# Two output projections of an adaptive block as three products of rounded halves, with the row products dealt out two and four to a turn

## The chip, the cores and the metric

The kernel runs on one core of one Trainium2 chip. The metric is the device time of one execution in microseconds (us), lower is better. Before the change it is 4800.77 us, the median of three runs (4797.85 to 4803.23 us).

## The reference, cut to what matters

Two transformer-like blocks over 512 tokens of width 1024 in fp32. The stage that is changed lies in the first block: the end of the token mixer and, beside it, the second block's first modulation vector, which only depends on a conditioning vector.

```python
y_att = attend(q, k, v) @ lw['w_attn_o']            # 512x1024 @ 1024x1024
y_conv = conformer_conv(u, lw)                      # its own projection is done earlier
merged = jax.nn.sigmoid(ga) * y_att + jax.nn.sigmoid(gc) * y_conv
return merged @ lw['w_out']                         # 512x1024 @ 1024x1024
...
xs = xs + g1 * token_mixer(hx, lw, rope, k_c, v_c)
hx = modulate(rmsnorm(xs, norm2_g[l]), sh2, sc2)    # begins with the mean of squares of xs
xs = xs + g2 * peer_ffn(hx, lw)
...
mod = (jnp.dot(cond, ada_w[layer]) + ada_b[layer])  # second block: 6144 values, each a dot product of length 1024
```

## The kernel before, in words

Activations lie channel by token: a tile of [128 channels, 8 groups, 512 tokens]. A projection to 1024 channels is eight slabs, one for each group of 128 outputs; a slab is a 128x1024 piece of the weight (512 KB), and its product is eight matmuls of 128x512 that add up in one PSUM bank. Slabs stream through a ring of four slots (`slab_ring`), filled by SyncE: it asks for slab n when the product of slab n - 4 has ended. `slab_used` counts ended products, `taken` counts banks that have been read, and four banks are in turn. Blocks of the program end with a barrier over all engines.

The stage is the function `mix_out` (from line 975). It has two phases of eight slabs each:

- Phase one, slabs 0 to 7 (`w_attn_o`): PE multiplies the attention's output `s.o` (the tile `conv`) by a slab (line 241). DVE multiplies the bank by one gate (line 1026) and adds the other branch (line 1028), and so makes group i of the merged tile.
- Phase two, slabs 8 to 15 (`w_out`): PE multiplies the merged tile by a slab. DVE scales the bank and adds it to x (line 1032), ACT squares the new group of x (line 1009), and PE sums the squares over channels (line 994, one matmul per group, two slabs behind).

Beside it DVE computes the second block's modulation: 48 row products, each the dot product of a 128x1024 tile of the transposed weight with a broadcast vector (`dot_row`, line 474, 512 KB of weight each). The rows come through a ring of four slots of their own (`mix_rows`), asked for by ACT (`fetch_row`, line 467): ACT waits until the row product that last used the slot has ended, then issues the DMA. Before the change three row products stand behind each slab in both phases. When the last of them has ended, DVE adds a bias and forms four small gain tiles (lines 480 and 495), and the block ends. The next block (the experts) begins with a square root on ACT (line 1305).

All instructions are issued in the order of the code, engine by engine. In other stages of this kernel projections are already done with halves: ACT rounds a slab to fp32r (`round_slab`, line 255), GpSimd subtracts that from the slab (`split_slabs`, line 262), the source is rounded and split in the same way on ACT and DVE (lines 269 and 276), and PE makes three fp32r products for each of the eight matmuls (`fine`, line 290; `fine_pair`, line 445, does two slabs at once as the source's groups arrive). `high` and `low` hold two slabs each.

Of the kernel before, what the change touches and what calls it, by code (L numbers as in the profile page):

```python
# [13 lines left out]
F32 = mybir.dt.float32  # L14
# [121 lines left out]
class Program:  # L136
# [838 lines left out]
    def mix_out(self, s):  # L975
# [3 lines left out]
        columns = list(range(NMOD))  # L979
        each = NMOD // (2 * KT)  # L980
        with self.nc.Block() as block:
# [5 lines left out]
            def _(pe):  # L987
                self.slabs(pe, 0, KT, self.linear(pe, s.o))
                pe.wait_ge(merged.sem, merged.at(KT))
                product = self.linear(pe, s.gates[:, KT:2 * KT, :])  # L990

# [3 lines left out]
                for i in range(KT):  # L995
                    pos = base + KT + i
                    pe.wait_ge(self.landed[pos % SLOTS], 16 * (pos // SLOTS + 1))
                    pe.wait_ge(self.taken, pos - SLOTS + 1)
                    product(pos % SLOTS, i).then_inc(self.slab_used, 1)
                    if i >= 2:  # L1000
                        square_sum(i - 2)
# [3 lines left out]
            @block.scalar  # L1005
            def _(act):
                def square(k):
                    act.wait_ge(self.taken, base + KT + k + 1)
                    act.activation(self.squares[:, k, :], self.x[:, k, :], ACT.Square).then_inc(squared.sem, 1)
                for n in range(NMOD):  # L1010
                    self.fetch_row(act, s, self.d["ada"], columns, n)
                    k, rest = divmod(n - each * KT - ROW_SLOTS + 1, each)
                    if k >= 0 and rest == 0:
                        square(k)
                for k in range((NMOD - ROW_SLOTS - each * KT) // each + 1, KT):
                    square(k)
                act.activation(self.one_root, self.eps[EPS], ACT.Sqrt)

            @block.vector
            def _(dve):  # L1020
                def rows(i):
                    for n in range(each * i, each * i + each):
                        self.dot_row(dve, s, n, self.crow[:, 1, :], self.mod2[:, columns[n]:columns[n] + 1])
                for i in range(KT):
                    dve.wait_ge(self.slab_used, base + i + 1)
                    dve.tensor_tensor(s.gates[:, i, :], self.bank[:, (base + i) % SLOTS, :], s.gates[:, i, :], ALU.mult).then_inc(self.taken, 1)
                    dve.wait_ge(self.taken, base + i + 1)
                    dve.tensor_tensor(s.gates[:, KT + i, :], s.gates[:, i, :], s.gates[:, KT + i, :], ALU.add).then_inc(merged.sem, 1)
                    rows(i)
                for i in range(KT):  # L1030
                    dve.wait_ge(self.slab_used, base + KT + i + 1)
                    dve.scalar_tensor_tensor(self.x[:, i, :], self.bank[:, (base + KT + i) % SLOTS, :], self.mod[:, 2 * KT + i, 0:1], self.x[:, i, :],
                                             ALU.mult, ALU.add).then_inc(self.taken, 1)
                    rows(KT + i)
                self.second_gains(dve, 0)
        merged.close(KT)
        squared.close(KT)
        self.close_rows(len(columns))
# [1506 lines left out]
    def build(self):  # L2545
        nc, d = self.nc, self.d
        with self.ctx:
# [44 lines left out]
            with ExitStack() as first:  # L2592
# [50 lines left out]
                with ExitStack() as inner:  # L2643
                    own = self.sb("mix_rows", [P, ROW_SLOTS, D], scope=inner)
                    s.mring = [own[:, j, :] for j in range(ROW_SLOTS)]
                    self.mix_out(s)
                if self.stop == "mixed":
# [325 lines left out]
```

## Time and profile before

| | us |
|---|---|
| median of three runs | 4800.77 |
| the profiled execution's own time | 4784.22 |
| its span (first to last instruction) | 4782.4 |
| the stage `mix_out`, from its first matmul to the end of DVE's last small gain | 606.7 to 727.8 |

The profiled execution is 16.6 us shorter than the median. A page of the profile lists busy time by engine, then groups of instructions by line. In a row of a group, `out<-in` names the tiles written and read, `xN` the count, the number after it the mean duration in ns, and what stands last is the idle time of the engine just before these instructions with what ended it. In a row of the timeline the first number is the start and the second the time to the end of the piece, both in us; instructions of one line are merged. The engines are PE (matmul), PEld (its weight load), DVE (VectorE), ACT (ScalarE), POOL (GpSimd), SP (SyncE); ACTq is ACT's queue issuing a DMA. An fp32 product of 128x512 shows as two records.

### The profile page before, as it was taken

Reading aid. Unit: us, or ns where it says so; the run is one execution under the profiler, and the core shown is the slowest. Engines: PE = TensorE matmul, PEld = TensorE weight load, DVE = VectorE, ACT = ScalarE, POOL = GpSimd, SP = SyncE. Lnnn points to the kernel's source line nnn. Section 1 sums busy time; section 2 is a strip of 40 time slices with the busy share of each in tenths; the row PEclk is TensorE's granted clock in tenths of the full one; section 3 lists DMA queues with packets and bytes.
Section 4 is the critical chain, followed back from the end, with each engine's and each line's share of the span. In section 5 each row is a group of like instructions: output and inputs, shape, how many; then the busy total and the mean of one; then the engine's idle time right before and its main releaser. Section 6 shows DMA issues by size and latency. Waiting matters only on the chain. (4 is left out here: it accounts for less than half of the span.)

```text
span 4782.4 us, 43840 instructions
## 1 busy us (share of the span) xinstructions
PE 4091.6 (86%) x15066; PEld 2742.5 (57%) x15066; DVE 2880.8 (60%) x4184; ACT 1659.3 (35%) x2193; POOL 1417.4 (30%) x1231
## 2 busy tenths in 40 slices
PE   4988997987776776777979999978999999999995
PEld 3874543432222322323767876767777877778774
DVE  4895656565656656652454456367557475574786
ACT  2322402222212212221324322326445364453675
POOL 0430003666666666664423442310000000000000
PEclk8998998999998998998989999988999999999998
DMA  4225076999999999997212364208658585675895
GB/s 153 94 86 202 1 266 236 376 383 368 364 370 371 370 377 365 365 373 272 84 49 71 96 216 149 88 18 350 260 214 306 190 319 208 227 288 190 326 362 199
DMA packets 260055, 1148.00 MB, mean 240 GB/s; under 512 B 28833, under 2 KB 28833, under 8 KB 212513
## 3 DMA queue, kind: packets, MB, share of 16 engines
q0 software_dynamic: 150768, 549.00, 30.0%
q1 hardware_dynamic: 87216, 514.37, 29.6%
q10 hardware_dynamic: 21888, 82.24, 4.7%
q8 instruction: 111, 1.82, 0.1%
q14 instruction: 72, 0.58, 0.0%
HBM read 1131.33 MB, written 14.16 MB: 240 GB/s over the span
## 5 line engine op out<-in xcount | busy, mean ns | idle before, releaser
L1417 PE MATMUL psum<-row,diag 128*128 128x512 f32 x1632 | 792.4, 632 | 274.0 <-DMA row<-in_peer_v,expert 157.0
L1417 PEld LDWEIGHTS psum<-row,diag 128*128 128x128 f32 x1632 | 312.7, 200 | 741.4 <-issue 451.3
L1248 DVE CUSTOM_DVE_ANT_0 row<-row,psum 128x1024 f32<-128x1024 f32 x412 | 496.9, 1218 | 290.4 <-DMA row<-in_peer_u,expert 250.6
L1215 POOL DMA_INDIRECT row<-in_peer_u,expert x412 | 390.5, 948 | 564.3 <-DVE expert L1161 428.3
L2258 PE MATMUL psum<-exp_high,exp_xt 128*128 128x512 f32 x1320 | 528.1, 400 | 26.2 <-DVE exp_low L2389 19.0
L2258 PE MATMUL psum<-exp_high,exp_xlow 128*128 128x512 f32 x1320 | 518.2, 393 | 0.0
L2258 PE MATMUL psum<-exp_low,exp_xt 128*128 128x512 f32 x1320 | 516.2, 391 | 0.0
L1215 POOL DMA_INDIRECT row<-in_peer_v,expert x408 | 384.9, 943 | 265.3 <-issue 111.2
L1329 ACT ACTIVATE diag<-consts_sb,coef 128x128 f32<-128x128 f32 x512 | 173.6, 392 | 626.7 <-remote 235.3
L2216 POOL COPY exp_number<-moe_slot_token 128x1 uint32 (+1 forms) x15 | 7.8, 521 | 1249.6 <-PE psum L2237 1203.1
L2258 PEld LDWEIGHTS psum<-exp_high,exp_xt 128*128 128x128 f32 x1320 | 249.0, 189 | 81.7 <-DVE exp_low L2389 21.7
L2258 PEld LDWEIGHTS psum<-exp_high,exp_xlow 128*128 128x128 f32 x1320 | 248.9, 189 | 53.9
L2258 PEld LDWEIGHTS psum<-exp_low,exp_xt 128*128 128x128 f32 x1320 | 249.6, 189 | 49.1
L2389 DVE TENSOR_TENSOR exp_low<-exp_wring,exp_high 128x2048 fp32r<-128x2048 f32 x99 | 225.4, 2291 | 86.3 <-ACT exp_high L2322 84.7
L2282 PE MATMUL psum<-exp_high,exp_ht 128*128 128x512 f32 x660 | 261.6, 396 | 13.2 <-DVE exp_htlow L2400 13.2
L2282 PE MATMUL psum<-exp_high,exp_htlow 128*128 128x512 f32 x660 | 261.2, 396 | 0.0
L2282 PE MATMUL psum<-exp_low,exp_ht 128*128 128x512 f32 x660 | 260.7, 395 | 0.0
L2322 ACT ACTIVATE exp_high<-exp_wring 128x2048 fp32r<-128x2048 f32 x99 | 188.2, 1912 | 51.7 <-PE psum L2282 46.9
L262 POOL TENSOR_TENSOR mix_low<-slab_ring,mix_high 128x1024 fp32r<-128x1024 f32 x48 | 119.1, 2484 | 230.2 <-ACT mix_high L255 230.2
L695 DVE SCALAR_TENSOR_TENSOR psum<-gpad,vectors_sb,psum 128x512 f32<-128x512 f32 x240 | 181.4, 756 | 8.6
L1417 PE MATMUL psum<-stat,diag 128*128 128x512 f32 x204 | 115.9, 697 | 82.6 <-DMA stat<-in_peer_v,expert 42.1
L2389 DVE TENSOR_TENSOR exp_low<-slab_ring,exp_high 128x2048 fp32r<-128x2048 f32 x66 | 151.2, 2291 | 51.8 <-ACT exp_high L2322 51.3
(495 smaller groups left out, 8093.4 us busy)
## 6 DMA issues: line engine op xcount, KB each, us to landing
exp_wring<-in_moe SPq DMA_DIRECT2D x99, 1024.0 KB, 6.5
h<-in_moe SPq DMA_DIRECT2D x66, 1024.0 KB, 6.0
squares<-in_moe SPq DMA_DIRECT2D x66, 1024.0 KB, 6.0
x<-in_moe SPq DMA_DIRECT2D x66, 1024.0 KB, 6.0
slab_ring<-in_moe SPq DMA_DIRECT2D x66, 1024.0 KB, 5.5
slab_ring<-in_w_in SPq DMA_DIRECT2D x92, 512.0 KB
mix_rows<-in_ada ACTq DMA_DIRECT2D x48, 512.0 KB, 5.1
squares<-in_ada ACTq DMA_DIRECT2D x48, 512.0 KB, 6.5
```

What stands on the lines that cost most here:

```text
L262: pool.tensor_tensor(s.low[:, i % 2, :], self.ring[(base + i) % SLOTS][:, 0:D], s.high[:, i % 2, :].bitcast(F32), ALU.subtract).then_inc(s ...
L695: dve.scalar_tensor_tensor(sum_, gp[:, tap:tap + T], self.vec("conv_w", TAPS * c + tap), sum_, ALU.mult, ALU.add).then_inc(tapped.sem, 1)
L1215: pool.indirect_dma_start(out=s.row[row % ROWS], out_offset=None, in_=table, in_offset=bass.IndirectOffsetOnAxis(ap=s.expert[:, g, j:j + 1 ...
L1248: dve.tensor_tensor_reduce(at, at, tokens[g // PH], 1.0, 0.0, ALU.mult, ALU.add, s.act[:, g % 2, j:j + 1]).then_inc(row_used.sem, 1)
L1329: act.activation(s.diag[:, number % DIAGS, :], self.const("ident"), ACT.Copy, scale=s.coef[:, g % 2, j:j + 1]).then_inc(lined.sem, 1)
L1417: mm = pe.matmul(sums[:, half * T:(half + 1) * T], s.diag[:, (PTOP * g + j) % DIAGS, :], s.row[row % ROWS][:, half * T:(half + 1) * T], st ...
L2216: pool.tensor_copy(s.number[:], s.slot_token[:, ds(place, 1)]).then_inc(numbered.sem, 1)
L2258: mm = pe.matmul(self.bank[:, buffers(of, c).start + u, :], xx[:, part * KT // 2 + k, :], w[:, at], start=part == 0 and k == 0 and n == 0, ...
L2282: mm = pe.matmul(self.side[:, 2 * u + half, :], x[:, m, kk * P:(kk + 1) * P], w[:, at], start=c == 0 and kk == 0 and n == 0, stop=c == STE ...
L2322: act.activation(s.high[:, i % ROUNDED, :], s.wring[i % MOE_SLOTS], ACT.Copy).then_inc(rounded.sem, 1)
L2389: dve.tensor_tensor(s.low[:, i % ROUNDED, :], s.wring[i % MOE_SLOTS], s.high[:, i % ROUNDED, :].bitcast(F32), ALU.subtract).then_inc(split ...
```

## The change

Both projections are done with halves: the source `s.o` is rounded by ACT and split by DVE before the first product, every slab is rounded by ACT (128x1024) and its low half is made by DVE (128x1024; elsewhere it is GpSimd), and every group of the merged tile is rounded by ACT and split by DVE as it is made. PE issues three fp32r matmuls where it had one in fp32. Slabs 0 and 1 are done as a pair. The row products are dealt out anew: two behind each slab of phase one and four behind each of phase two, 48 as before.

```diff
--- before.py
+++ after.py
@@ -977,7 +977,14 @@
         base = self.used
         merged, squared, summed = self.sig("merged"), self.sig("squared"), self.sig("summed")
         columns = list(range(NMOD))
-        each = NMOD // (2 * KT)
+        rounded, split, slab_split = self.sig("h_rounded"), self.sig("h_split"), self.sig("slab_split")
+        slab_rounded = self.sig("slab_rounded")
+        FIRST, SECOND = 2, 4
+        assert KT * (FIRST + SECOND) == NMOD
+
+        def numbers(i):
+
+            return range(FIRST * i, FIRST * i + FIRST) if i < KT else range(FIRST * KT + SECOND * (i - KT), FIRST * KT + SECOND * (i - KT + 1))
         with self.nc.Block() as block:
             @block.sync
             def _(sp):
@@ -985,16 +992,16 @@
 
             @block.tensor
             def _(pe):
-                self.slabs(pe, 0, KT, self.linear(pe, s.o))
-                pe.wait_ge(merged.sem, merged.at(KT))
-                product = self.linear(pe, s.gates[:, KT:2 * KT, :])
+                self.fine_pair(pe, s)
+                self.fine_rest(pe, s)
+                self.slabs(pe, SLOTS, KT - SLOTS, self.fine(pe, s, SLOTS, ready=None))
+                product = self.fine(pe, s, KT, source=(s.mhigh, s.mlow), ready=KT)
 
                 def square_sum(k):
                     pe.wait_ge(squared.sem, squared.at(k + 1))
                     return pe.matmul(self.side[:, 0, :], self.const("ones"), self.squares[:, k, :], start=k == 0, stop=k == KT - 1)
                 for i in range(KT):
                     pos = base + KT + i
-                    pe.wait_ge(self.landed[pos % SLOTS], 16 * (pos // SLOTS + 1))
                     pe.wait_ge(self.taken, pos - SLOTS + 1)
                     product(pos % SLOTS, i).then_inc(self.slab_used, 1)
                     if i >= 2:
@@ -1007,33 +1014,56 @@
                 def square(k):
                     act.wait_ge(self.taken, base + KT + k + 1)
                     act.activation(self.squares[:, k, :], self.x[:, k, :], ACT.Square).then_inc(squared.sem, 1)
-                for n in range(NMOD):
+                for i in range(2):
+                    self.round_slab(act, s, base, i)
+                self.round_source(act, s, s.o)
+                for n in range(ROW_SLOTS):
                     self.fetch_row(act, s, self.d["ada"], columns, n)
-                    k, rest = divmod(n - each * KT - ROW_SLOTS + 1, each)
-                    if k >= 0 and rest == 0:
-                        square(k)
-                for k in range((NMOD - ROW_SLOTS - each * KT) // each + 1, KT):
-                    square(k)
+                for i in range(2 * KT):
+                    if i + 2 < 2 * KT:
+                        self.round_slab(act, s, base, i + 2)
+                    if i < KT:
+                        act.wait_ge(merged.sem, merged.at(i + 1))
+                        act.activation(s.mhigh[:, i, :], s.gates[:, KT + i, :], ACT.Copy).then_inc(rounded.sem, 1)
+                    else:
+                        square(i - KT)
+                    for n in numbers(i):
+                        if n + ROW_SLOTS < NMOD:
+                            self.fetch_row(act, s, self.d["ada"], columns, n + ROW_SLOTS)
                 act.activation(self.one_root, self.eps[EPS], ACT.Sqrt)
 
             @block.vector
             def _(dve):
                 def rows(i):
-                    for n in range(each * i, each * i + each):
+                    for n in numbers(i):
                         self.dot_row(dve, s, n, self.crow[:, 1, :], self.mod2[:, columns[n]:columns[n] + 1])
+
+                def low_slab(i):
+                    dve.wait_ge(slab_rounded.sem, slab_rounded.at(i + 1))
+                    dve.tensor_tensor(s.low[:, i % 2, :], self.ring[(base + i) % SLOTS][:, 0:D], s.high[:, i % 2, :].bitcast(F32),
+                                      ALU.subtract).then_inc(slab_split.sem, 1)
+                low_slab(0)
+                low_slab(1)
+                self.split_source(dve, s, s.o)
                 for i in range(KT):
                     dve.wait_ge(self.slab_used, base + i + 1)
+                    low_slab(i + 2)
                     dve.tensor_tensor(s.gates[:, i, :], self.bank[:, (base + i) % SLOTS, :], s.gates[:, i, :], ALU.mult).then_inc(self.taken, 1)
                     dve.wait_ge(self.taken, base + i + 1)
                     dve.tensor_tensor(s.gates[:, KT + i, :], s.gates[:, i, :], s.gates[:, KT + i, :], ALU.add).then_inc(merged.sem, 1)
                     rows(i)
+                    dve.wait_ge(rounded.sem, rounded.at(KT + i + 1))
+                    dve.tensor_tensor(s.mlow[:, i, :], s.gates[:, KT + i, :], s.mhigh[:, i, :].bitcast(F32), ALU.subtract).then_inc(split.sem, 1)
                 for i in range(KT):
                     dve.wait_ge(self.slab_used, base + KT + i + 1)
+                    if i + 2 < KT:
+                        low_slab(KT + i + 2)
                     dve.scalar_tensor_tensor(self.x[:, i, :], self.bank[:, (base + KT + i) % SLOTS, :], self.mod[:, 2 * KT + i, 0:1], self.x[:, i, :],
                                              ALU.mult, ALU.add).then_inc(self.taken, 1)
                     rows(KT + i)
                 self.second_gains(dve, 0)
         merged.close(KT)
+        self.close_split(2 * KT, 2)
         squared.close(KT)
         self.close_rows(len(columns))
         self.sig("cooked").close(4)
@@ -2643,6 +2673,11 @@
                 with ExitStack() as inner:
                     own = self.sb("mix_rows", [P, ROW_SLOTS, D], scope=inner)
                     s.mring = [own[:, j, :] for j in range(ROW_SLOTS)]
+                    s.high = self.sb("out_high", [P, 2, D], F32R, scope=inner)
+                    s.low = self.sb("out_low", [P, 2, D], F32R, scope=inner)
+                    s.hhigh, s.hlow = self.over("out_hhigh", self.h, [P, KT, T]), self.over("out_hlow", s.o, [P, KT, T])
+                    halves = self.over("merged_halves", s.gates, [P, 2 * KT, T])
+                    s.mhigh, s.mlow = halves[:, 0:KT, :], halves[:, KT:2 * KT, :]
                     self.mix_out(s)
                 if self.stop == "mixed":
                     return self.dump(self.x[:])
```

`round_slab`, `round_source`, `split_source`, `fine`, `fine_pair` and `fine_rest` are as in the listing above.

What ACT issues in phase two stands here as the program has it, before the change. `squares<-x` is the squaring of a group of x, `DMA mix_rows` a row's fetch, which waits for a row product (`row_dotted`).

```order
L467 DMA mix_rows<-in_ada 128x1024 [waits row_dotted] x24
L1009 ACTIVATE squares<-x 128x512 [waits bank_taken]
L467 DMA mix_rows<-in_ada 128x1024 [waits row_dotted] x3
L1009 ACTIVATE squares<-x 128x512 [waits bank_taken]
L467 DMA mix_rows<-in_ada 128x1024 [waits row_dotted] x3
```

The same engine after the change, from the end of the attention into phase one and, after the dots, at the passage into phase two. `out_high<-slab_ring` rounds a slab, `merged_halves<-gates` a merged group.

```order
L255 ACTIVATE out_high<-slab_ring 128x1024 [waits slab_landed0]
L255 ACTIVATE out_high<-slab_ring 128x1024 [waits slab_landed1]
L269 ACTIVATE out_hhigh<-conv 128x512 x8
L467 DMA mix_rows<-in_ada 128x1024 x4
L255 ACTIVATE out_high<-slab_ring 128x1024 [waits slab_used,slab_landed2]
L1027 ACTIVATE merged_halves<-gates 128x512 [waits merged]
L467 DMA mix_rows<-in_ada 128x1024 [waits row_dotted] x2
...
L255 ACTIVATE out_high<-slab_ring 128x1024 [waits slab_used,slab_landed2]
L1016 ACTIVATE squares<-x 128x512 [waits bank_taken]
L467 DMA mix_rows<-in_ada 128x1024 [waits row_dotted] x4
```

A slab's rounding now stands behind the fetches of the turn before, so ACT reaches it only when that turn's last row product has ended.

DVE before the change, one turn of phase one and the start of the next:

```order
L1026 TENSOR_TENSOR gates<-psum,gates 128x512 [waits slab_used]
L1028 TENSOR_TENSOR gates<-gates 128x512 [waits bank_taken]
L474 ISA mix_rows,mod<-mix_rows,cond_rows 128x1024 [waits row_slab_landed0]
L474 ISA mod 128x1
L474 ISA mix_rows,mod<-mix_rows,cond_rows 128x1024 [waits row_slab_landed1]
L474 ISA mod 128x1
L474 ISA mix_rows,mod<-mix_rows,cond_rows 128x1024 [waits row_slab_landed2]
L474 ISA mod 128x1
```

DVE after the change, one turn of phase one (`out_low<-slab_ring` is a slab's low half, the last row a merged group's):

```order
L1043 TENSOR_TENSOR out_low<-slab_ring,out_high 128x1024 [waits slab_rounded,slab_used]
L1051 TENSOR_TENSOR gates<-psum,gates 128x512
L1053 TENSOR_TENSOR gates<-gates 128x512 [waits bank_taken]
L474 ISA mix_rows,mod<-mix_rows,cond_rows 128x1024 [waits row_slab_landed0]
L474 ISA mod 128x1
L474 ISA mix_rows,mod<-mix_rows,cond_rows 128x1024 [waits row_slab_landed1]
L474 ISA mod 128x1
L1056 TENSOR_TENSOR merged_halves<-gates,merged_halves 128x512 [waits h_rounded]
```

The low half of the slab after next comes first in a turn, ahead of the reading of the bank, and a turn of phase two is the same with line 1061 in the place of lines 1051 and 1053, four row products, and no merged group.

## Rows read from the trace of the kernel before

**Rows 1.** Two stretches: us, busy PE, PEld, DVE, ACT, POOL, granted clock, DMA share, GB/s.
```profile
615.00:663.00 48.00, 46.89 (x110) 20.47 (x108) 33.67 (x57) 0.00 (x0) 0.00 (x0) 1.00 0.87 294
670.00:722.00 52.00, 52.00 (x123) 23.06 (x122) 29.27 (x49) 4.41 (x7) 0.00 (x0) 1.00 0.85 279
```
**Rows 2.** DVE's bank readers of both phases: ns min/median/max, first and last start.
```profile
L1026 DVE TENSOR_TENSOR gates<-psum,gates x8: 692/692/692, 613.9 to 661.9; 128x512 f32<-128x512 f32 x8
...
L1032 DVE SCALAR_TENSOR_TENSOR x<-psum,mod,x x8: 751/751/752, 670.6 to 722.9; 128x512 f32<-128x512 f32 x8
```
**Rows 3.** Timeline: the first fetch and the first product of the stage.
```profile
606.32 2.58 ACTq L467 DMA_DIRECT2D mix_rows<-in_ada  x4
...
606.69 0.69 PE L241 MATMUL psum<-conv,slab_ring 128*128 128x512 f32 x1 [1.28 <-PEq L776]
```
**Rows 4.** Timeline, DVE in a turn of each phase.
```profile
620.72 0.69 DVE L1026 TENSOR_TENSOR gates<-psum,gates 128x512 f32<-128x512 f32 x1 [2.01 <-PE psum L241]
621.45 0.69 DVE L1028 TENSOR_TENSOR gates<-gates 128x512 f32<-128x512 f32 x1
622.06 1.22 DVE L474 CUSTOM_DVE_ANT_0 mix_rows<-mix_rows,cond_rows 128x1024 f32<-128x1024 f32 x1
...
670.57 0.75 DVE L1032 SCALAR_TENSOR_TENSOR x<-psum,mod,x 128x512 f32<-128x512 f32 x1 [3.79 <-PE psum L241]
671.24 1.22 DVE L474 CUSTOM_DVE_ANT_0 mix_rows<-mix_rows,cond_rows 128x1024 f32<-128x1024 f32 x1
...
673.52 1.22 DVE L474 CUSTOM_DVE_ANT_0 mix_rows<-mix_rows,cond_rows 128x1024 f32<-128x1024 f32 x1
```
**Rows 5.** Timeline, DVE's last row product of the stage, and the next block.
```profile
725.88 1.22 DVE L474 CUSTOM_DVE_ANT_0 mix_rows<-mix_rows,cond_rows 128x1024 f32<-128x1024 f32 x1
...
728.08 0.69 ACT L1305 ACTIVATE stat<-psum,eps 128x512 f32<-128x512 f32 x1 [2.22 <-PEq L981]
```
**Rows 6.** Timeline, PE in a warm stage of half products.
```profile
200.02 0.39 PE L290 MATMUL psum<-in_hlow,in_high 128*128 128x512 f32 x1
200.25 0.39 PE L290 MATMUL psum<-in_hhigh,in_high 128*128 128x512 f32 x1
```
**Rows 7.** DVE making low halves, two sizes, from the lines of the whole span.
```profile
L2389 DVE TENSOR_TENSOR exp_low<-exp_wring,exp_high 128x2048 fp32r<-128x2048 f32 x99 | 225.4, 2291 | 86.3 <-ACT exp_high L2322 84.7
...
L418 DVE TENSOR_TENSOR ffn_hlow<-h,ffn_hhigh 128x512 fp32r<-128x512 f32 x8 | 5.5, 693 | 2.9 <-ACT ffn_hhigh L396 2.5
```
**Rows 8.** Timeline of a half-products stage that starts from rest (PE, ACT, POOL).
```profile
2466.15 2.00 ACT L255 ACTIVATE res_high<-slab_ring 128x1024 fp32r<-128x1024 f32 x2 [18.37 <-PEq L1643]
2468.06 4.25 ACT L269 ACTIVATE res_hhigh<-y 128x512 fp32r<-128x512 f32 x8
...
2474.47 0.63 PE L290 MATMUL psum<-res_hhigh,res_high 128*128 128x512 f32 x1
2474.90 0.63 PE L290 MATMUL psum<-res_hhigh,res_low 128*128 128x512 f32 x1
...
2479.60 1.06 ACT L255 ACTIVATE res_high<-slab_ring 128x1024 fp32r<-128x1024 f32 x1 [7.29 <-PE psum L290]
...
2480.74 2.52 POOL L262 TENSOR_TENSOR res_low<-slab_ring,res_high 128x1024 fp32r<-128x1024 f32 x1 [8.32 <-ACT res_high L255]
```
**Rows 9.** The first 5.7 us of PE's work in that stage, in the columns of Rows 1.
```profile
2470.00:2475.70 5.70, 4.30 (x9) 2.98 (x10) 5.70 (x7) 2.31 (x5) 2.42 (x1) 0.50 0.00 0
```
**Rows 10.** Timeline of ACT: the fetch behind the row product of 673.52.
```profile
674.78 0.33 ACTq L467 DMA_DIRECT2D mix_rows<-in_ada  x1
```
**Rows 11.** Landing of rows here, and in a later stage with larger slabs.
```profile
DMA to landing us min/median/max: 3.5/5.1/6.5
...
squares<-in_ada ACTq DMA_DIRECT2D x46, 512.0 KB, 6.5
```
**Rows 12.** Stretches of the attention's end, in the columns of Rows 1.
```profile
585.00:595.00 10.00, 8.21 (x31) 4.34 (x29) 4.04 (x12) 3.63 (x7) 0.00 (x0) 1.00 0.01 2
595.00:605.00 10.00, 8.53 (x19) 4.13 (x18) 1.09 (x3) 1.19 (x2) 0.00 (x0) 0.66 0.00 0
```

## The prediction

> **What bounds the kernel now.** The change touches one stage of some 121 us out of 4782, so I read the views of that stage only. The table of stretches comes first: in phase one PE is busy 46.89 of 48 us and in phase two 52.00 of 52, at a granted clock of 1.00, while DVE has 33.67 and 29.27 us of work and ACT almost none; the DMA engines are busy 0.87 and 0.85 of the time [rows 1]. PE sets the pace. The readers of the banks show it: eight starts of line 1026 from 613.9 to 661.9 are seven turns of 6.86 us, which is eight fp32 products of 0.86 us; line 1032 starts from 670.6 to 722.9, 7.47 us a turn, since from the third slab on one more product, a sum of squares, stands in each turn [rows 2]. The first product starts at 606.69, after 1.28 us of rest for PE [rows 3]. DVE waits 2.01 us for PE in a turn of phase one and 3.79 us before the first of phase two [rows 4]. The stage's end is DVE's: its last row product starts at 725.88, and 2.2 us later the next block begins with a square root at 728.08 [rows 5]. Whatever happens inside the stage, the time follows the start of that last row product.
>
> **What the change takes from PE.** In a warm stage of half products the records start 0.23 us apart (200.02 and 200.25), so a slab is 24 x 0.231 = 5.54 us against 6.86 [rows 6]. That is 1.3 us a slab, 21 us over sixteen, if PE still set the pace. It doesn't.
>
> The Trainium skill, TensorE: Matmul & The Clock Gate, "Back-to-back issue gap", gives a sustained stream of N=512 products about 131 ns each; the measured spacing here is 0.23 us. By that figure the opening pair below would be 4.5 us shorter (45 x 0.10) and the whole change +4.6 instead of +9.1; the measurement decides.
>
> **What it gives to DVE and ACT.** DVE's low half of a slab is 128x1024; the trace has 693 ns at 128x512 and 2291 ns at 128x2048 [rows 7], so on the line between them 1.23 us, and about 1.15 us from start to start, as a row product of 1.22 us is followed by the next after 1.14 us [rows 4]. Sixteen of them are 18 us of DVE. ACT rounds a slab in 1.06 us, and the engine that makes the low half starts 1.14 us after ACT did (2479.60, 2480.74) [rows 8]. The row products are 48 as before.
>
> *The opening.* ACT issued its first fetch at 606.32 [rows 3]; in place of it, it now rounds slab 0 from about 606.35. From rest, two slabs and the first group of the source take it 1.91 us to the source's start (2466.15 to 2468.06) [rows 8], so the source starts at 608.26. DVE makes low halves at 607.49 and 608.64, splits group 0 at 609.79 for 0.69, and PE starts at 610.6, 3.9 later than now. The pair has 48 products; slab 0 ends after 45 of them, 10.4 us, plus 0.16 for the last one to drain (records of 0.39 at a spacing of 0.23): 621.15. PE has then rested from 605.4 to 610.6. In the stage that starts from rest the granted clock was 0.50 for the first 5.7 us and nine products [rows 9], spaced 0.43 (2474.47, 2474.90) [rows 8]; I take the same nine, 9 x 0.196 = 1.8 us (bounds: nothing, or twice that). Slab 0 ends at 622.9. Then ACT rounds slab 2, and DVE starts its low half 1.19 us later (0.05 for the wait, 1.14 as above): turn 0 of DVE starts at 624.1. Its bank is read at 625.3, where it is now read at 613.9.
>
> *A turn of phase one.* On ACT the rounding of slab i+2 stands behind the fetches of turn i-1, the last of which waits for that turn's last row product. On DVE that slab's low half is first in turn i. So each turn closes a circle: the last row product ends, ACT issues a fetch 0.04 us later for 0.33 us (673.52 + 1.22, then 674.78) [rows 10], goes on to the rounding after 0.07 (an estimate), and 1.14 us later DVE starts. That is 1.58 us; from below it could be 1.14, were the fetch to cost ACT nothing. From a turn's start the low half takes 1.15, line 1051 0.73 and line 1053 0.61 to the next (620.72, 621.45, 622.06), the first row product 1.14 and the second 1.22 [rows 4]: 4.85, and with 1.58 it is 6.43 us. The split of the merged group (0.69, ending at 5.46) lies in the 1.58 and costs nothing; uncovered, eight of them would cost 5. PE needs 5.54 and waits 0.9 a turn for a low half. ACT's rounding of the merged group (0.6) lies beside the row products. Seven turns: turn 7 starts at 624.1 + 45.0 = 669.1.
>
> *The passage.* Slab 8 needs the last merged group: split at 669.1 + 5.46 = 674.6, then three products and the drain, 0.9 with the wait: 675.5. ACT rounds slab 10 only now, so turn 8 starts at 676.7.
>
> *A turn of phase two.* 1.15 for the low half, 0.67 for line 1061 (670.57 to 671.24), three row products at 1.14 and one of 1.22 [rows 4], and 1.58: 8.06 us (7.6 with the lower bound of the circle), against 7.47 now. PE needs 5.54 + 0.86 and is covered. Turns 8 to 13 have a low half; turn 13 starts at 676.7 + 40.3 = 717.0 and its row products at 718.8. In turns 14 and 15 there is none, and DVE could go on after 5.3 us, but a slot's next row is asked for when its product ends and lands 5.1 us later by the median [rows 11]: 1.22 + 0.04 + 5.1 + 0.05 = 6.4 us from one turn's row products to the next. They start at 725.2 and 731.6, the last one at 731.6 + 3.4 = 735.0.
>
> *The sum.* 735.0 - 725.9 = +9.1 us. In other words the first reading of a bank comes 11.4 later, seven turns of phase one give back 0.43 each (3.0), the passage 1.1 and the last two turns 1.5, and the turns in between, five of 8.06 where two of 6.86 and three of 7.72 stood, cost 3.4. The profiled execution's own time goes from 4784.2 to 4793.3; the runs' median, 16.6 us above it, from 4800.8 to 4809.9, say **4810**.
>
> Nothing else carries a cost. SyncE's refills are in the same order and have two turns, 12 us, between a slot's release and its use, against 5.1 to land. The squares on ACT stand between a rounding and the fetches, ahead of the first row product's end. POOL rests in this stage. What follows begins as now: PE rests over 8 us before the experts in either kernel.
>
> **Rivals.**
> *PE keeps the pace.* If ACT's rounding did not stand in the circle, DVE's turn of phase one would be 5.46 and PE's 5.6, and phase two's 6.5. For it: DVE is busy only 0.7 and 0.56 of the time now [rows 1]. Against: the order of ACT's instructions. Turn 7 would start at 663.3, turn 8 at 670.9, turn 13 at 703.3, and with the two last turns at 6.4 the last row product at 721.4: 4.5 us less than now, 4796, not slower. It decides where the rounding is ready before the last row product has ended.
> *Rows come late.* Phase two moves five transfers of 0.52 MB in 8.06 us, 325 GB/s, the four rows within 3.4 us of each other, where the stage now runs at 279 to 294 [rows 1]. A later stage at such loads lands its rows in 6.5 us [rows 11]. Up to 6.7 is hidden in turns 9 to 13, but the two last grow by 1.4 each: +12. At 7.2 us of landing a turn is 8.5: five turns by 0.44 and two by 2.1, +15.6, 4816.
> *PE at its lower clock.* The attention's end shows both sides: 8.21 of 10 us busy at a clock of 1.00, then 8.53 of 10 busy at 0.66 [rows 12]. PE will be busy 86% and 79%, with a rest in each turn. Were the clock at the lower level throughout, a slab would take 24 x 0.427 = 10.2 us and with the sum of squares 12: six turns by 3.8 and eight by 3.9, +54 on top, 4864. Against it: the rests are 0.9 and 1.7 us, and the clock held 1.00 up to 595 with rests of that size. The Trainium skill, on the same page under "A second HAM failure mode: psum-queue depth-cycling", says that short rests between groups of matmuls that cycle through PSUM banks can make the clock swing; that would be this case, and the first of these two rows disagrees.
>
> **Chances.** The circle sets the pace: 0.55, its own range 4805 to 4815 (the clock at the start 1.8 either way, the circle 0.44 x 12 below, landing 1.4 x 2 above). Late rows 0.2. PE keeps the pace 0.15. The lower clock 0.05. Something in the experts that gains from a shifted start 0.05. What a measurement of this kernel can tell from no change is about 0.2%, 9.6 us, and the forecast lies on that line: slower by more, half of the first case, the late rows and the clock, 0.52; within it, the other half and PE's pace, 0.42; faster by more, 0.06. The range is 4796 to 4820, which leaves out the clock and a part of the ends.
>
> **What would show it.** In the changed profile: PE's first product at 610.6, at a clock of 0.5 for some us; DVE's bank readings 6.4 us apart in phase one and 8.06 in phase two, each turn's low half waiting for ACT's rounding, and ACT's rounding starting 0.4 us after the last row product; PE waiting for low halves about 0.9 and 1.7 us a turn; the row products of the last two turns waiting for DMA; the next block's square root at 737. The forecast is wrong if DVE's low half waits for nothing, if the turns are 5.6 us, or if the granted clock falls inside the phases.

## The result, and the profile after

The changed kernel takes 4817.95 us (median of 14 runs, 4804.85 to 4825.97) beside 4799.73 us (median of 14, 4794.58 to 4806.47). The ratio is 1.0034, 95% interval 1.0026 to 1.0043, so 12.5 to 20.6 us slower. The forecast was 4810 in a range of 4796 to 4820, with slower the likelier side at 0.52. So the time lies 2 us inside the upper end of the range, and the change, +18.2, is twice the +9.1 that was added up. The profiled execution of the changed kernel took 4818.04 us.

The opening of the stage in the timeline, which answers to [rows 3]:

```profile
612.25 1.06 ACT L255 ACTIVATE out_high<-slab_ring 128x1024 fp32r<-128x1024 f32 x1 [0.28 <-PEq L776]
...
616.45 0.77 PE L445 MATMUL psum<-out_hhigh,out_high 128*128 128x512 f32 x1 [5.12 <-DVE out_hlow L276]
...
631.10 1.22 DVE L1043 TENSOR_TENSOR out_low<-slab_ring,out_high 128x1024 fp32r<-128x1024 f32 x1 [10.58 <-ACT out_high L255]
```

This execution came to the stage 5.9 us later than the one before the change (612.25 against 606.32), in code that is the same; so the stage is measured from its own start. PE's first product is 4.20 us behind ACT's first rounding, and DVE, which had rested 10.58 us, begins turn 0 at +18.85. The readers of the banks, which answer to [rows 2]:

```profile
L1051 DVE TENSOR_TENSOR gates<-psum,gates x8: 681/681/683, 632.2 to 677.8; 128x512 f32<-128x512 f32 x8
...
L1061 DVE SCALAR_TENSOR_TENSOR x<-psum,mod,x x8: 742/744/746, 686.2 to 740.5; 128x512 f32<-128x512 f32 x8
```

The first takes seven turns in 45.6 us, 6.51 each (6.75, then 6.47), where it was 6.87; the second 54.3 us, 7.76 each, where it was 7.47. One turn of phase one, for [rows 4], DVE first and then ACT:

```profile
641.46 1.22 DVE L474 CUSTOM_DVE_ANT_0 mix_rows<-mix_rows,cond_rows 128x1024 f32<-128x1024 f32 x1
642.61 0.08 DVE L474 DVE_READ_ACCUMULATOR2_ANT mod<- 128x1 f32 x1
642.61 0.69 DVE L1056 TENSOR_TENSOR merged_halves<-gates,merged_halves 128x512 fp32r<-128x512 f32 x1
644.32 1.22 DVE L1043 TENSOR_TENSOR out_low<-slab_ring,out_high 128x1024 fp32r<-128x1024 f32 x1 [1.03 <-ACT out_high L255]
```
```profile
641.57 1.48 ACTq L467 DMA_DIRECT2D mix_rows<-in_ada  x2
643.15 1.06 ACT L255 ACTIVATE out_high<-slab_ring 128x1024 fp32r<-128x1024 f32 x1 [2.09 <-DVE mod L474]
```

The row product ends at 642.68, the second fetch's issue at 643.05, ACT rounds at 643.15, DVE makes the low half at 644.32. This way from DVE's row product over ACT's fetch and rounding back to DVE is called the corner below. It takes 1.64 us; DVE splits the merged group in the first part of it and rests for 1.03 us, and ACT's rest is put down to the row product. The end of the stage, for [rows 5], with the row products that waited:

```profile
703.70 1.23 DVE L474 CUSTOM_DVE_ANT_0 mix_rows<-mix_rows,cond_rows 128x1024 f32<-128x1024 f32 x1 [0.56 <-DMA mix_rows<-in_ada]
...
708.30 1.22 DVE L474 CUSTOM_DVE_ANT_0 mix_rows<-mix_rows,cond_rows 128x1024 f32<-128x1024 f32 x1 [0.81 <-DMA mix_rows<-in_ada]
...
736.76 1.22 DVE L474 CUSTOM_DVE_ANT_0 mix_rows<-mix_rows,cond_rows 128x1024 f32<-128x1024 f32 x1 [0.66 <-DMA mix_rows<-in_ada]
...
745.92 1.23 DVE L474 CUSTOM_DVE_ANT_0 mix_rows<-mix_rows,cond_rows 128x1024 f32<-128x1024 f32 x1
```
```profile
748.12 0.69 ACT L1335 ACTIVATE stat<-psum,eps 128x512 f32<-128x512 f32 x1 [4.66 <-PEq L988]
```

Six row products wait for DMA, 3.3 us in all, two of them in turn 10. From ACT's or DVE's first instruction of the stage to the last row product it is 133.7 us, where it was 119.6 (606.3 to 725.9): +14.1. The landing, for [rows 11], and the stretches, for [rows 1] and [rows 9]:

```profile
DMA to landing us min/median/max: 3.4/5.0/8.6
```
```profile
632.00:683.00 51.00, 42.40 (x167) 32.36 (x168) 42.36 (x64) 12.49 (x15) 0.00 (x0) 0.94 0.72 230
685.00:741.00 56.00, 45.64 (x180) 33.78 (x178) 45.09 (x70) 9.72 (x12) 0.00 (x0) 0.96 0.88 309
617.00:622.00 5.00, 5.00 (x13) 3.92 (x12) 3.52 (x6) 1.42 (x3) 0.00 (x0) 0.50 0.48 194
```

PE is no longer full: 42.40 of 51 and 45.64 of 56 us. The slowest row landed in 8.6 us where it was 6.5. PE's granted clock is below 1.00 in both long stretches. It fell at two rests of PE, in phase one and at the passage:

```profile
632.47 0.74 PE L290 MATMUL psum<-out_hhigh,out_high 128*128 128x512 f32 x1 [1.93 <-DVE out_low L1043]
...
682.17 0.80 PE L290 MATMUL psum<-merged_halves,out_high 128*128 128x512 f32 x1 [5.49 <-DVE merged_halves L1056]
```
```profile
632.00:636.00 4.00, 3.53 (x9) 2.82 (x10) 3.96 (x8) 0.63 (x1) 0.00 (x0) 0.57 0.56 201
680.00:690.00 10.00, 7.83 (x24) 6.32 (x25) 7.04 (x12) 1.69 (x2) 0.00 (x0) 0.66 0.60 179
```

### The profile page after: what moved, and what is told of

Read it like the earlier page. It is cut to its first block and busy times, and to the rows that moved or that the text cites. A ratio compares the mean times of both kernels' runs of the same rounds, so it can differ in the third digit from the quotient of the medians.

```text
span 4816.2 us, 44180 instructions
## 1 busy us (share of the span) xinstructions
PE 4084.0 (85%) x15194; PEld 2774.1 (58%) x15194; DVE 2901.6 (60%) x4216; ACT 1686.0 (35%) x2225; POOL 1419.8 (29%) x1231
## 5 line engine op out<-in xcount | busy, mean ns | idle before, releaser
L2419 DVE TENSOR_TENSOR exp_low<-h,exp_high 128x2048 fp32r<-128x2048 f32 x66 | 150.3, 2291 | 49.6 <-ACT exp_high L2352 48.5
```

The source lines that it names most:

```text
L2419: dve.tensor_tensor(s.low[:, i % ROUNDED, :], s.wring[i % MOE_SLOTS], s.high[:, i % ROUNDED, :].bitcast(F32), ALU.subtract).then_inc(split ...
```

## Experiments

"Stage" is the time from ACT's first instruction in it (a rounding or a fetch) to the start of DVE's last row product. "First bank" is DVE's first reading of a bank after that start; the passage lies between the last reading of phase one and the first of phase two. "Turns of phase two" are the five from turn 8 to turn 13; the two last turns have no low half and are left out. The last column is the ratio to the kernel before on the same chip, with its 95% interval. These chips run the whole kernel in some 4665 us instead of 4800.

| kernel | first bank | turn of phase one | passage | turns of phase two | stage | ratio |
|---|---|---|---|---|---|---|
| before | 7.5 | 6.87 | 8.64 | 6.87, 7.72 | 119.6 | |
| before_again | 7.5 | 6.87 | 8.64 | 6.87, 7.72 | 119.6 | |
| changed | 20.0 | 6.47 | 8.41 | 8.09, once 9.91 | 133.7 | 1.0034 (1.0026 to 1.0043) |
| again | 19.7 | 6.47 | 8.41 | 8.09, once 9.66 | 133.1 | 1.0039 (1.0025 to 1.0053) |
| round_first | 19.8 | 5.35 | 8.41 | 7.5 to 8.4, once 7.0 | 122.7 | 1.0003 (0.9994 to 1.0012) |
| spin | 17.4 | 6.47 | 8.40 | 8.09, once 8.54 | 130.4 | 1.0027 (1.0017 to 1.0037) |
| three_three | 20.2 | 7.62 | 9.55 | 6.95 | 132.4 | 1.0028 (1.0019 to 1.0037) |
| eight_slots | 20.0 | 5.35 | 7.72 | 6.95 | 114.5 | 0.9991 (0.9982 to 1.0) |
| up_front | 22.5 | 5.35 to 5.63 | 7.72 | 5.8 to 7.0 | 114.8 | 0.9991 (0.9981 to 1.0001) |
| up_front_eight | 20.2 | 5.35 to 5.89 | 8.26 | 5.8 to 6.5 | 112.1 | 0.9988 (0.9978 to 0.9997) |
| dealing_only | 7.5 | 6.87 | 8.64 | 6.87, 7.72 | 120.7 | 1.0004 (0.9995 to 1.0013) |
| gpsimd_low | 19.0 | 6.42 | 8.21 | 7.4 to 8.4 | 131.9 | 1.0028 (1.0016 to 1.004) |
| tuned | 17.7 | 5.35 | 6.22 | 5.2 to 6.4 | 104.5 | 0.9965 (0.9951 to 0.9978) |

### again and before_again: where the loss is

Nothing is altered in either.

> The changed kernel once more, nothing altered: which part of its excess comes back. In the two profiles the stage from ACT's first instruction to the start of DVE's last row product is 119.6 us before (606.3 to 725.9) and 133.7 us after (612.3 to 745.9), +14.1; the stretch of the experts between DVE's last small gain and the first rounding of the next stage is 1543 us before and 1553 after. Theory (the whole loss is in the stage): the stage comes back at 133 to 135 us, the experts' stretch scatters about 1543 to 1553, and the median is 12 to 18 us above before. Rival (part of the loss is in the experts): their stretch is again 1550 or more.

> The kernel before, unaltered, for its stage and its experts' stretch on the same chip as the others. On an earlier chip the stretch from the last row product to the first rounding of the next stage was 1419.3, 1419.2, 1419.0 and 1417.3 us in the changed kernel and three variants. Theory (nothing outside the stage is touched): the stage is 119.6 us, and the stretch equals that of the three others of this group within 2 us. Rival (the experts start differently and lose): the stretch before is 3 us or more shorter than in the three others.

The changed stage comes back to 0.6 us, the one before to less than 0.1. The experts' stretch does not: from the next block's square root to the first rounding of the stage behind the experts it was 1542.7 us in the profile before and 1552.6 in the one after, but on the other chips 1417.0 (again), 1417.7 (before_again), 1415.0 (three_three), 1416.6 (dealing_only), and all of the eleven lie between 1414.6 and 1417.7. Between the two profiled executions of the first pair lie 33.8 us: 5.9 ahead of the stage, 14.1 in it, 9.8 in the experts' stretch and 3.9 behind it. The 9.8 belong to that pair, not to the change. The theory that the loss is in the stage stands; the medians, 18.2 and 17.3 us, are 4 us above the stage's 14.1 and 13.5, inside their intervals.

### round_first: the circle

```diff
+                late = []
                 for i in range(2 * KT):
                     if i + 2 < 2 * KT:
                         self.round_slab(act, s, base, i + 2)
+                    for n in late:
+                        if n + ROW_SLOTS < NMOD:
+                            self.fetch_row(act, s, self.d["ada"], columns, n + ROW_SLOTS)
...
-                    for n in numbers(i):
+                    keep = 2 if i < KT else 1
+                    late = list(numbers(i))[-keep:]
+                    for n in list(numbers(i))[:-keep]:
```

> ACT rounds the slab after next before the last fetches of the turn before: ahead of both in phase one, ahead of the last one in phase two. Nothing else is altered. Theory (the circle of last row product, fetch, rounding and low half sets the turns): phase one goes from 6.47 to PE's 5.5 or 5.6 us a turn and phase two from 8.09 to about 6.95, 12 us less in the stage, so a median 11 to 13 us below the changed kernel, at 4805 or so. Rival (rows that come late, or the DMA engines, set phase two): phase one gains its 6 us, phase two gains nothing or little, since row products then wait for DMA; 6 us in all. Rival (the circle is not what paces): no change of the turns at all.

```profile
L1060 DVE TENSOR_TENSOR gates<-psum,gates x8: 678/682/685, 625.7 to 663.2; 128x512 f32<-128x512 f32 x8
...
L1070 DVE SCALAR_TENSOR_TENSOR x<-psum,mod,x x8: 743/744/746, 671.6 to 724.1; 128x512 f32<-128x512 f32 x8
```
```profile
700.91 1.23 DVE L474 CUSTOM_DVE_ANT_0 mix_rows<-mix_rows,cond_rows 128x1024 f32<-128x1024 f32 x1 [1.11 <-DMA mix_rows<-in_ada]
```

Seven turns of phase one take 37.5 us, 5.35 each: DVE's own instructions and nothing else. Order of issue alone is worth 1.1 us a turn there, 7.8 in all, and 10.4 in the stage. Phase two gains less than the theory had: twelve row products now wait for DMA, up to 1.66 us, and 7.7 in all. Circle and late rows are both real, one behind the other.

### eight_slots: the late rows

This is added to `round_first`; the four more slots lie in `qk`, a tile of the attention that is dead by then.

```diff
-                    own = self.sb("mix_rows", [P, ROW_SLOTS, D], scope=inner)
-                    s.mring = [own[:, j, :] for j in range(ROW_SLOTS)]
+                    globals()["ROW_SLOTS"] = 8
+                    own = self.sb("mix_rows", [P, 4, D], scope=inner)
+                    s.mring = [own[:, j, :] for j in range(4)]
+                    s.mring += [s.qk[:, 2 * j:2 * j + 2, :].rearrange("p a n -> p (a n)") for j in range(ROW_SLOTS - 4)]
```

> As the kernel that rounds first, and the ring of rows has eight slots instead of four (four more in a tile that is dead by then). Rounding first brought phase one to 5.35 us a turn, but phase two stayed at 7.0 to 8.4 a turn with nine or more row products waiting for DMA, 0.2 to 1.7 us each. Theory (a row is asked for only when its slot's last product has ended, and 5 to 7.5 us of landing do not fit into a turn of 6.95): with eight slots every row is there, phase two runs at 6.9 to 7.0 us a turn, the stage is 115 to 117 us instead of 122.7, and the median 6 to 7 us below the one that rounds first. Rival (the DMA engines are full: 2.62 MB a turn at the 327 GB/s seen there is 8.0 us): phase two stays at 7.5 or more and the stage at 120 or more.

No row product waits for DMA, and phase two runs at 6.95 a turn. The stage is 114.5 us, 8.2 less, with five transfers in 6.95 us (377 GB/s): the DMA engines had not been full at the 327 GB/s of the expectation, the ring was too short for the landing. Of the 8.2 us, 0.7 are at the passage (7.72 instead of 8.41) and aren't the ring's: PE rests 2.9 us there in both, and its granted clock is at the lower level behind it in `round_first` and not here.

### spin: the lower clock at the opening

```diff
             @block.tensor
             def _(pe):
+                self.spin(pe, 9)
                 self.fine_pair(pe, s)
```

> PE does nine products of 128x256 into an unused bank before the pair, from the barrier until the source's first halves are there, so that it does not rest. Theory (the lower clock at the opening costs 14 products x 0.196 = 2.7 us): the pair runs at a spacing of 0.23 from its first product, turn 0 of DVE starts 2.7 us earlier (16.1 instead of 18.85 us after ACT's start), and all turns behind it by the same. Rival (the opening is bound by ACT and DVE halving the source): the spacing is 0.23 but the pair waits for groups and turn 0 starts less than 1 us earlier.

The stretch from 605 to 625 us in `again` and here (columns as in Rows 1):

```profile
605.00:625.00 20.00, 13.83 (x48) 10.75 (x48) 7.81 (x11) 7.72 (x12) 0.00 (x0) 0.83 0.35 118
```
```profile
605.00:625.00 20.00, 17.08 (x72) 13.25 (x72) 9.65 (x14) 7.82 (x12) 0.00 (x0) 1.00 0.43 149
```

The granted clock is 1.00 in this stretch, the first bank is read 2.3 us earlier (2.7 by the theory) and the stage is 2.7 shorter. Of these, 2.3 are shown to be the clock's; the rest lies where rows come late (turn 10 took 8.54 instead of 9.66, and the last turns took longer), which differs from run to run. The turns of phase one do not change, as they are not PE's.

### three_three and dealing_only: what the dealing is worth

```diff
-        FIRST, SECOND = 2, 4
+        FIRST, SECOND = 3, 3
```

> Row products dealt out three and three instead of two and four, nothing else altered. Theory (DVE's turn is its own instructions plus the circle's 1.6 us): phase one 6.47 + 1.15 = 7.6 us a turn, phase two 8.09 - 1.15 = 6.95 a turn, no row comes late, the last turns are shorter by 1 to 2 us each; the sum in the stage -1 to +2 us. Rival (rows that come late cost more than the two places seen): 4 us or more is gained in the stage. Rival (PE paces phase one): phase one stays below 6.6 a turn and the stage gains 7 us or more.

The turns are 7.62 and 6.95, as DVE's instructions and the corner give; the stage is 0.7 us shorter than in `again`. One row product more or less is one 1.15 us more or less a turn, and no dealing of this kind helps while each turn has its corner.

The other is the kernel before with the new dealing, all in fp32:

```diff
-                for n in range(NMOD):
-                    self.fetch_row(act, s, self.d["ada"], columns, n)
...
+                for n in range(ROW_SLOTS):
+                    self.fetch_row(act, s, self.d["ada"], columns, n)
+                for i in range(2 * KT):
+                    if i >= KT:
+                        square(i - KT)
+                    for n in numbers(i):
+                        if n + ROW_SLOTS < NMOD:
+                            self.fetch_row(act, s, self.d["ada"], columns, n + ROW_SLOTS)
```

> The kernel before with nothing but the new dealing of row products, two and four a turn; both projections stay in fp32. Theory (PE paces with 6.86 and 7.73 us a turn, and the dealing shows only behind the last slab, where four row products stand instead of three): the stage goes from 119.6 to 120.7 us, the median is within 3 us of before. Rival (rows that come late reach this kernel too, since four a turn must be asked for within 5.3 us): a wait for DMA before the last turn's row products, stage 121.5 to 123.

The stage is 120.7, +1.15, one row product behind the last slab. Two row products wait for DMA (0.73 and 0.54 us) and cost nothing, since PE paces. Of the change's +14.1 the dealing by itself is 1.1; the halves, with the place that ACT gives their rounding, bring the rest.

### gpsimd_low: another engine for the low halves

```diff
+            @block.gpsimd
+            def _(pool):
+                self.split_slabs(pool, s, base, 2 * KT)
...
-                low_slab(0)
-                low_slab(1)
...
-                    low_slab(i + 2)
```

> The changed kernel with the low halves of the slabs made by GpSimd, as the other stages do, instead of DVE; DVE keeps the source's and the merged groups'. Theory (the circle is what paces, and it loses DVE's 1.15 us a slab but the low half itself takes GpSimd 2.4 us beside DVE): the turns become PE's, 5.6 us in phase one, and 6.4 to 7 in phase two, unless the two engines slow each other: in the stage of the residual DVE's 128x512 additions take 2.77 us beside GpSimd and 0.69 alone, and then a turn gains little. Expected stage 124 to 130 us against 133.4, median 4 to 9 us below the changed kernel. Rival (DVE slowed by GpSimd loses more than the 1.15 us): stage 133 or more, no gain or a loss.

```profile
642.04 3.43 DVE L474 CUSTOM_DVE_ANT_0 mix_rows<-mix_rows,cond_rows 128x1024 f32<-128x1024 f32 x1
```
```profile
641.80 2.59 POOL L262 TENSOR_TENSOR out_low<-slab_ring,out_high 128x1024 fp32r<-128x1024 f32 x1 [2.70 <-ACT out_high L255]
```

The forecast of 124 to 130 missed: the stage is 131.9. DVE's row product beside GpSimd's subtraction takes 3.43 us instead of 1.22. DVE no longer rests in a turn of phase one: its own 5.35 us, less 1.15 for the low half, plus 2.2 for the slower row product, are 6.4, which is the turn (6.42). The rival was nearer. The stage is 1.2 us shorter than in `again`, and the ratios' intervals overlap, so in this order of ACT's neither engine is shown to be the better one. GpSimd in the order of `round_first` was not run; there a turn of 6.4 would stand against DVE's 5.35, an estimate from these two runs.

### up_front, up_front_eight and tuned: using DVE's rest at the opening

The first, beside spin and the later fetches (one a turn):

```diff
-        FIRST, SECOND = 2, 4
-        assert KT * (FIRST + SECOND) == NMOD
+        UP, FIRST, SECOND = 8, 2, 3
+        assert UP + KT * (FIRST + SECOND) == NMOD
...
-                for n in range(ROW_SLOTS):
+                for n in range(ROW_SLOTS + UP):
...
                 self.split_source(dve, s, s.o)
+                for n in range(UP):
+                    self.dot_row(dve, s, n, self.crow[:, 1, :], self.mod2[:, columns[n]:columns[n] + 1])
```

> Everything found so far in one: PE spins at the opening, ACT rounds a slab before the last fetch of the turn before, and eight row products are done while PE works at the pair, when DVE rested 10.6 us; then two a turn in phase one and three in phase two. Four slots of rows. Theory (DVE's idle time at the opening is the one place where row products are free, and with 3 a turn PE paces phase two at 5.54 + 0.86 = 6.4 us): first bank read 17.4 us after ACT's start or earlier, phase one 5.4 to 5.6 a turn, passage 8.4, phase two 6.4 a turn, stage 104 to 108 us against 119.6 before: a median 10 to 14 us below before. Rival (rows come late there too): phase two at 7 us a turn or more, stage 112 or more.

> As the one with eight row products up front, with eight slots of rows. Theory: if rows come late with four slots, these 1 to 5 us go; stage 104 to 106 us. Rival (PE paces already): the same stage within 1 us.

Both miss: 114.8 and 112.1 us where 104 to 108 and 104 to 106 were forecast. The first bank is read at 22.5 and 20.2 instead of 17.4: I had made the mistake of the change itself once more. ACT's first twelve or sixteen fetches stood ahead of slab 2's rounding, and the last of them waited for the eighth row product. PE rested 7.1 and 4.8 us for it, and the granted clock was at the lower level for 6.8 us around the end of that rest. With four slots the rival held too: eight row products waited for DMA, 8.55 us in all, and with eight slots none. In `up_front_eight`:

```profile
625.47 1.22 DVE L474 CUSTOM_DVE_ANT_0 qk<-qk,cond_rows 128x1024 f32<-128x1024 f32 x1
...
628.33 1.22 DVE L1054 TENSOR_TENSOR out_low<-slab_ring,out_high 128x1024 fp32r<-128x1024 f32 x1 [1.63 <-ACT out_high L255]
```

In the last kernel five are up front, their slots' fetches stand behind slab 2's rounding, two fetches a turn stand behind a rounding, and the last merged group is split before turn 7's row products. It has eight slots and the spin, as above.

```diff
+        UP, COUNTS = 5, [2] * KT + [4, 4, 4, 3, 3, 3, 3, 3]
...
+                late = list(range(UP))
...
-                    rows(i)
+                    if i < KT - 1:
+                        rows(i)
                     dve.wait_ge(rounded.sem, rounded.at(KT + i + 1))
...
+                    if i == KT - 1:
+                        rows(i)
```

> All that the runs pointed to: PE spins at the opening; five row products while PE works at the pair, then two a turn in phase one and 4, 4, 4, 3, 3, 3, 3, 3 in phase two; eight slots of rows; the rounding of a slab ahead of the last two fetches of the turn before, that of slab 2 ahead of all fetches that wait; and the last merged group is split before turn 7's row products. Theory: first bank read 17.4 to 18 us after ACT's start (20.2 and 22.5 with eight row products up front, whose fetches ACT put ahead of slab 2's rounding), phase one 5.4 to 5.6 a turn, passage 6.6 instead of 8.3, phase two 6.4 on average, stage 107 to 111 us, median 8 to 12 us below before. Rival (PE's granted clock falls more often as its turns fill and empty): stage 113 or more.

Its stretches in both phases, the readers of the banks and the last row product:

```profile
625.00:665.00 40.00, 37.79 (x163) 30.42 (x163) 38.91 (x58) 11.96 (x15) 0.00 (x0) 1.00 0.91 338
670.00:716.00 46.00, 43.52 (x177) 32.76 (x175) 43.44 (x73) 11.87 (x15) 0.00 (x0) 1.00 0.85 330
```
```profile
L1064 DVE TENSOR_TENSOR gates<-psum,gates x8: 680/683/689, 627.0 to 664.5; 128x512 f32<-128x512 f32 x8
...
L1077 DVE SCALAR_TENSOR_TENSOR x<-psum,mod,x x8: 742/744/751, 670.7 to 710.9; 128x512 f32<-128x512 f32 x8
```
```profile
713.88 1.22 DVE L474 CUSTOM_DVE_ANT_0 qk<-qk,cond_rows 128x1024 f32<-128x1024 f32 x1
```

The stage is 104.5 us, 15.0 less than before and shorter than the 107 to 111 expected, and the kernel takes 4648.4 us beside 4665.0: 0.9965 (0.9951 to 0.9978). PE and DVE are busy 0.94 to 0.97 of the time and DMA 0.91 and 0.85, and the clock is 1.00. It beats the kernel before, with the same products in halves. So the loss was not in the halves but in the order, the ring and the opening; what each of the last edits is worth by itself was not run.

## Why the prediction was right, and where its sum was short

The direction, the place and the mechanism were right; the sum was +9.1 and the stage gave +14.1.

- *PE's gain does not count.* Right: PE's spacing of 0.23 in the warm part of the pair is as in [rows 6], and PE rests 0.6 us in a turn of phase one (1.93 in turn 0) and 1.5 in one of phase two (2.63 behind turn 10). The 131 ns that the Trainium skill, TensorE: Matmul & The Clock Gate, "Back-to-back issue gap", gives for a sustained product is not what this trace shows.
- *The opening.* PE's first product came at +4.20 us (4.25 forecast), turn 0 at +18.85 (17.75). The term that was mis-sized is the lower clock: 14 products at 0.43 instead of nine, 2.7 us instead of 1.8; `spin` reads the first bank 2.3 us earlier.
- *The circle.* 1.64 us instead of 1.58, and 1.9 in turn 0; seven turns 45.6 instead of 45.0. `round_first` shows it to be the cause in phase one: without it 5.35 a turn. In phase two it takes `eight_slots` as well to show it, 6.95 instead of 8.09.
- *The passage.* From turn 7 to turn 8 it was 8.40 instead of 7.6. PE rested 5.49 us for the last merged group and did the last products at the lower clock, which the forecast had only for the opening.
- *Phase two.* 8.09 a turn as against 8.06 (whose terms add up to 8.04), but turn 10 took 9.91, its last row landing 8.6 us after its issue began. Here the step "Up to 6.7 is hidden in turns 9 to 13" met rows that landed in up to 8.6 us. From turn 8 to 13 it is 42.3 instead of 40.3, and from there to the last row product 18.6 instead of 18.0.
- The five differences, 1.1 + 0.6 + 0.8 + 2.0 + 0.6, are the missing 5. All have one sign, and with the medians' further 4 us the sum was half of what was measured; that the time still lies in the range, 2 us from its end, is in part luck. The rival of late rows, given 0.2, thus held in part, for some 2.5 us, beside the circle and not instead of it. The rival of PE's pace fell: no turn was 5.6.
- *The rival of the lower clock.* It does not make the turns, but the clock did fall inside the phases, which the prediction had named as a sign that it is wrong. Behind PE's rest of 1.93 us in turn 0 it was at the lower level from 632.5 to 635.9, for eight products, and at the passage from 680.3 to 687.1; these make the 0.94 and, with the last sums, the 0.96 of the stretches. The first cost nothing in the turns, as PE had a rest to give: turn 0 took 6.75 us, and 6.76 in `again`, where the clock stayed at 1.00 behind the same rest. The argument from [rows 12] was also weaker than it looked: that trace has a rest of 1.79 us just ahead of its fall at 595. The swing of the clock behind short rests that the Trainium skill, TensorE: Matmul & The Clock Gate, "A second HAM failure mode: psum-queue depth-cycling", tells of appeared once in phase one, behind the 1.93 us, and not behind the rests of 0.6, 1.5 and 2.63 us.
- The medians lie 4 us above what the stage gives, on both occasions inside the interval. What they are, if anything, stays open. Single profiles can't tell: the time behind the experts alone differs by 12 us among the eleven later ones (2511.8 to 2524.0).

## What to carry to other kernels

Before an engine's product is made faster, look at the instruction that must feed it, and at what stands ahead of that instruction on its engine: a rounding placed behind a fetch that waits for the consumer's last piece of side work puts the whole turn on one chain, and moving it ahead was worth 10 us here with no instruction less. Then side work goes where its engine rests anyway (an opening in which it waits 10 us), with its fetches behind the roundings that the main path waits for (`up_front` had them ahead and lost 5 us at the opening), and its ring has to be as long as the landing at the load that the faster loop makes, not at the old one.

## What the hardware showed that was not expected

- A DVE product-and-sum of 128x1024 took 3.43 us while GpSimd did a subtraction of 128x1024 (2.59 us), and 1.22 alone.
- In the changed kernel PE's rests of 5.1 us (opening) and 5.5 us (passage) each went with 6.8 us at the lower clock, in both of its executions that were profiled. Behind shorter rests one execution differed from the next: behind the same 1.93 us the clock fell for 3.4 us in the first profile and in `three_three`, and not in `again`, `round_first` and `spin`; behind 2.86 us it fell for 6.8 us in `round_first`, and behind 2.85 us not in `eight_slots`. What decides it is not shown.
- ACT's queue issued the first fetches, which wait for nothing, at 612.53, while its first rounding still ran (612.25 to 613.31): an issue that had nothing to wait for did not wait for the engine's work ahead of it.
- The changed kernel's stage took 133.7 us in the first profile and 133.1 on another chip, while the experts' stretch, with its gathers, took 1543 and 1553 us in the first pair of profiles and 1415 to 1418 on the three later chips.
